# One weight piece of a mixture-of-experts stream loaded by nine transfers instead of one

## The reference

```python
def expert_block(args):
    xb, e = args
    g = xb @ w_gate[e] + b_gate[e]
    u = xb @ w_up[e] + b_up[e]
    g = jnp.minimum(g, SWIGLU_LIMIT)
    u = jnp.clip(u, -SWIGLU_LIMIT, SWIGLU_LIMIT)
    a = g * jax.nn.sigmoid(SWIGLU_ALPHA * g) * (u + 1.0)
    return a @ w_down[e] + b_down[e]
```

## Time and profile before

| what | us |
|---|---|
| median of 3 runs (1153.05 to 1154.56) | 1153.4 |
| the profiled execution, its own time | 1153.93 |
| the profiled execution, its span from first to last instruction | 1152.1 |
| TensorE busy in it (94% of the span) | 1081.1 |
| VectorE busy, ScalarE busy | 307.8, 212.9 |
| moved by DMA | 439.53 MB, mean 382 GB/s |

### The profile page before, as it was taken

How to read it: one execution, slowest core, us unless ns; L and a number is a source line. 1 busy time by engine, 2 the same in 40 slices (tenths; PEclk the granted TensorE clock), 3 DMA queues, 4 the chain that set the end, 5 groups by cost and what they waited for, 6 DMA issues and landing times.

```text
span 1152.1 us, 12104 instructions
## 1 busy us (share of the span) xinstructions
PE 1081.1 (94%) x5226; PEld 499.7 (43%) x5226; DVE 307.8 (27%) x690; ACT 212.9 (18%) x365; POOL 3.6 (0%) x11
## 2 busy tenths in 40 slices
PE   7999989999999999999999999999999898999997
PEld 6888879733333333333333333333333333333332
DVE  7566667531111112111111111111111111111122
ACT  5345445311111111111111111111111111000102
POOL 0000000000000000000000000000000000000000
PEclk9999999999999999999999999999999999999999
DMA  9754228799999999999999999999999999999995
GB/s 356 256 177 153 108 76 318 332 416 427 428 427 428 427 428 427 428 427 428 428 427 428 428 427 427 428 428 427 428 428 427 427 427 428 429 428 427 428 427 240
DMA packets 44858, 439.53 MB, mean 382 GB/s; under 512 B 3946, under 2 KB 5506, under 8 KB 20228
## 3 DMA queue, kind: packets, MB, share of 16 engines
q1 hardware_dynamic: 44788, 438.74, 91.2%
q10 hardware_dynamic: 16, 0.00, 0.0%
HBM read 437.68 MB, written 1.05 MB: 381 GB/s over the span
## 4 chain that ended last, share of the span: by engine, by line
PE 62%; DMA 31%; DVE 3%; issue 2%; ACT 1%; SPq 0%; DVEq 0%; ACTq 0%
PE ps L1006 37%; DMA pool<-in_w_up_dram 23%; DMA pool<-in_w_down_dram 4%; DMA attn<-in_w_up_dram 4%; PE ps L665 4%; PE ps L1028 3%; PE ps L937 3%; PE ps L695 2%; PE ps L746 2%; PE ps L703 2%; PE ps L993 1%; PE ps L799 1%; PE ps L801 1%; PE ps L800 1%; DMA wu<-in_w_in_dram 1%
## 5 line engine op out<-in xcount | busy, mean ns | idle before, releaser
L1006 PE MATMUL ps<-pool,o_t 128*64 128x512 f32 x2144 | 482.6, 596 | 31.9 <-DMA pool<-in_w_gate_dram 12.0
L1006 PEld LDWEIGHTS ps<-pool,o_t 128*64 128x64 f32 x2144 | 153.6, 137 | 319.2 <-issue 275.4
L1438 DVE TENSOR_SCALAR v_tok<-ps 128x512 f32<-128x512 f32 x32 | 22.1, 692 | 504.3 <-PE ps L1006 504.3
L1006 PE MATMUL ps<-attn,o_t 128*64 128x512 f32 x320 | 72.5, 594 | 4.1 <-DMA attn<-in_w_gate_dram 3.4
L599 ACT ACTIVATE o_t<-ps 128x512 f32<-128x512 f32 x32 | 19.1, 597 | 305.7 <-PE ps L665 305.6
L606 ACT ACTIVATE attn<-ps 64x512 f32<-64x512 f32 x60 | 35.5, 591 | 217.1 <-PE ps L1006 216.4
L1006 PE MATMUL ps<-slot_wv,o_t 128*64 128x512 f32 x304 | 69.4, 598 | 4.3 <-issue 2.2
L1006 PE MATMUL ps<-slot_gt,o_t 128*64 128x512 f32 x304 | 69.4, 598 | 4.3 <-issue 2.2
L586 ACT ACTIVATE attn<-v_tok 128x512 f32<-128x512 f32 x32 | 20.2, 630 | 243.1 <-DVE v_tok L1438 243.1
L1028 PE MATMUL ps<-attn,o_t 128*128 128x512 f32 x128 | 60.3, 594 | 0.8 <-DVE attn L1506 0.8
L937 PE MATMUL ps<-xs,work 128*64 128x512 f32 x256 | 60.7, 593 | 0.2 <-DVE work L1374 0.2
(11 more groups left out here) (190 smaller groups left out, 962.9 us busy)
## 6 DMA issues: line engine op xcount, KB each, us to landing
pool<-in_w_gate_dram SPq DMA_DIRECT2D x45, 2048.0 KB, 39.3
pool<-in_w_up_dram SPq DMA_DIRECT2D x45, 2048.0 KB, 39.4
pool<-in_w_down_dram SPq DMA_DIRECT2D x44, 2048.0 KB, 39.4
attn<-in_w_gate_dram SPq DMA_DIRECT2D x7, 2048.0 KB, 39.5
slot_wv<-in_w_up_dram SPq DMA_DIRECT2D x7, 2048.0 KB, 37.2
slot_gt<-in_w_down_dram SPq DMA_DIRECT2D x7, 2048.0 KB, 42.9
slot_gt<-in_w_up_dram SPq DMA_DIRECT2D x6, 2048.0 KB, 34.5
attn<-in_w_down_dram SPq DMA_DIRECT2D x6, 2048.0 KB, 38.3
```

Of the source, the lines that this page charges most:

```text
L1006: mm = pe.matmul(ps[SLOTS * h:SLOTS * h + SLOTS, bank, :], lhs[:, k, :], ring[n % RING][:, r, 512 * h:512 * h + 512], start=(k == 0 and no ...
L1438: dve.tensor_scalar(g_act, ps[:, G, :], LIMIT, None, ALU.min).then_inc(g_ready, 1)
```

## The change

Piece 96 is loaded by nine transfers in place of one: one of 64 partitions, then eight of 8 partitions each, all on SyncE's queue, into the same slot and with the same semaphore. The bytes and their places are the same. Each of the nine raises the semaphore by 16, so this slot's semaphore goes up by 144 for piece 96 instead of 16, and the waits for piece 96 and for all later pieces of slot 6 ask for 128 more. No other piece, and nothing on TensorE, VectorE or ScalarE, is changed.

```diff
+        EVEN_OUT = 96
+
+        def landed(n):
+            return 16 * (n // RING + 1) + (16 * 8 if n % RING == EVEN_OUT % RING and n >= EVEN_OUT else 0)
+
...
+                elif n == EVEN_OUT:
+                    expert, m, j = ORDER[n]
+                    sp.dma_start(ring[n % RING][0:P // 2], expert_v[m][expert, j, 0:P // 2]).then_inc(ld_ring[n % RING], 16)
+                    for p in range(P // 2, P, 8):
+                        sp.dma_start(ring[n % RING][p:p + 8], expert_v[m][expert, j, p:p + 8]).then_inc(ld_ring[n % RING], 16)
...
-                        pe.wait_ge(ld_ring[n % RING], (n // RING + 1 if again is None else again + (n // RING + 1)) * 16)
+                        pe.wait_ge(ld_ring[n % RING], landed(n) if again is None else again * 16 + landed(n))
```

## The result

The kernel with piece 96 in nine transfers takes 1168.32 us (median of 4 runs, 1168.09 to 1169.37), against 1153.98 us of the kernel before on the same chip: ratio 1.0127, 95% interval 1.0111 to 1.0143. I had predicted 1153.0, range 1151.6 to 1155.9, and 0.14 for slower by more than 2.3 us. It is 14.3 us slower by the medians, 14.7 by the ratio.

What follows compares the result with a forecast made beforehand. The landing of the last pieces through the full DMA queue was taken as the bound. All other terms being 0, 1153.93 - 0.35 = 1153.6 us profiled, 0.53 above the median, gave 1153.05, stated as 1153.0; range 1151.6 to 1155.9.

Steps and rivals of the forecast that it cites:

- What bounds the kernel: End of the kernel: landing of the last weight pieces sets it, through a full DMA queue moving 428 GB/s.
- Where the bytes go: Piece 96: one half of the engines carries 12 packets, the other 4, where both carried 8.
- Four packets at 26.7 GB/s, 2.45 us: From piece 96 on: four packets, 65.5 KB, shift one half of the engines 2.45 us earlier, the other 2.45 us later.
- Which half is late?: End of the stream: narrow transfers' engines were taken to be ahead, so piece 96 relieves the late half; -0.35 us, chance 0.58.
- one spot at the beginning: At 27.3 us, narrow transfers follow a 2 MB one; the engines they use were ahead, those left out last.
- the prediction's own last sentence: Wrong if engine lag isn't kept from 680 us, or if the slowest engine at the end is one narrow transfers use.
- The rival: End of the stream: the late half gets the bytes and ends 2.45 us later, time 1155.85; chance 0.18.
- -0.35 us: End of the stream: late engines relieved, but an early-half straggler becomes slowest, 1140.1 to 1139.75; range -0.8 to 0.
- Nine issues fit, the queue doesn't run dry: SyncE at piece 96: nine issues, 2.95 us, fit in 3.43 us and can't empty the queue; 0 us.
- Piece 96 itself, 0 us: Piece 96's use at 675.22: it lands up to 2.45 us later, any TensorE wait replacing a later one; 0 us.

Runs made afterwards that it cites:

- twice is twice: Pieces 96 and 126 each loaded in two transfers of 64 neighbouring partitions, against the kernel before: ratio 1.0150, cost 17.3 us.
- 64 or 32 neighbours: Piece 96 in two transfers of 64 neighbouring partitions, or four of 32, against the kernel before: ratio 1.0067 or 1.0081.
- every 8th: Piece 96 in eight transfers of 16 partitions, each taking every 8th of all 128, against the kernel before: ratio 1.0068, cost 7.8 us.
- every 4th of all 128: Piece 96 in four transfers of 32 partitions, each taking every 4th, against the kernel before: ratio 0.9998, cost 0 us.
- the run with 16 neighbours: Piece 96 in eight transfers of 16 neighbouring partitions, against the kernel before: ratio 1.0093, cost 10.7 us.
- free loadings: Piece 96 in four every-4th transfers, or only its lower half in eight narrow every-4th transfers, against the kernel before: ratio 0.9998 or 1.0005.
- eight column pieces: Piece 96 in eight transfers of all 128 partitions, 512 columns of one row each, against the kernel before: ratio 1.0010, cost 1.2 us.

## Why the prediction was wrong, point by point

*What bounds the kernel* held: the stream of pieces sets the end, what it loses at piece 96 is lost for good, and twice is twice.

*Where the bytes go* held in the count: from 640 to 700 us the kernel after has 226 packets under 512 B, 16 for each of its 10.1 pieces and 64 more, as one for each of eight engines in each of the eight narrow transfers makes.

*Four packets at 26.7 GB/s, 2.45 us* is the step that failed. It priced a packet by the engine alone and took for granted that an engine writes at the same rate to whatever partition. The trace of before had no transfer in the full stream that wasn't spread over all 128 partitions, so nothing there showed another price. A price that the trace doesn't show has to be bounded from both sides; a lower rate for the 64 neighbours and for the narrow ones belonged in the range, and I had put it at nothing. Measured: the rate fell from 427 to 226 GB/s for 21 us, and 10.2 of the 14.7 us are lost rate.

The Trainium skill had the rule, and I had looked past it: "SBUF — State Buffer", section "Door 1: The DMA port swizzle (why `[64,N]` ≈ `[32,N]`)", says that the rate depends on how many of 16 ports the partitions of a transfer reach, that 4 neighbours share a port with the 4 that lie 32 further, and that 64 neighbours reach no more ports than 32. By it 64 or 32 neighbours, and every 8th, reach half of the ports and every 4th of all 128 reaches all; the runs agree (7.4 to 8.0 us lost against 0, the dip at 197 to 249 GB/s of 427). A quarter of the ports should be slower still, and the run with 16 neighbours (8.8 us) says hardly. In the free loadings each engine can have a port by itself; in all costly ones several have to meet at one. That is how the runs read together with the page; no view names engines or ports, so it is argued, not shown.

*Which half is late?* Read from one spot at the beginning, and half right. Most late engines are relieved by the change, but the latest is one that gets the four packets; by the prediction's own last sentence that alone makes it wrong. The rival said that one such engine is enough, and so it was: in place of -0.35 us the distance of the last engine from a level end grew by 3.3 us in the change. Its price, 2.45 us, was near. I gave it 0.18, and it came on top of the loss of rate, which I hadn't at all.

*Nine issues fit, the queue doesn't run dry* held, and for far more than was asked: 27 us of issues cost 1.2 us (0 to 2.2).

*Piece 96 itself, 0 us*: TensorE waited 8 us for it, in place of later waits, as I had argued; the price was in the stream.

Left open: whether it is the writing side alone, which no run parts from reading over the whole piece; why bytes of the pieces beside piece 96 slow down too; why a quarter of the places is hardly worse than a half (engines at work on different ones of the eight transfers at one time would reach more places; no run tests it); what makes half of the engines late by the end; and why the narrow transfers of the upper half lose about as much by neighbours as by every 4th (10.3 or 9.4 us) while in the lower half it is 5.4 or 0. A gentler levelling isn't in sight: if the places belong to the engines as argued above, each narrow transfer that takes bytes off the other eight engines has to write their partitions.

## What to carry to other kernels

Keep every transfer of a DMA-bound stream spread over all 128 partitions; if a piece has to be cut, cut its columns, or take every 4th partition, not blocks of neighbours: the same four transfers cost 9 us or nothing. Every 8th isn't enough, it costs 7.8 us. In the profile look at the DMA share and the GB/s together: here a share of 1 with half the GB/s was a stream at half its speed with no engine idle. And before bytes are moved between engines to level an end, show that the latest engine is among those relieved; one that isn't takes the whole gain.

## What the runs showed of the hardware

- A cut of one 2 MB piece of 439.53 MB into two halves of 64 neighbouring partitions slows the whole queue to half its rate for 15 us (two halves, 197 to 249 GB/s), and the cut of the change for some 20 us (mean 226 GB/s); cut by every 4th partition it goes on at 427 GB/s.
- Transfers of 8 partitions use eight engines (64 completion packets for eight of them), and by every 4th partition of the lower half they don't slow the stream (428 GB/s over all), while by every 4th of the upper half they do (374 GB/s from 640 to 700 us).
- With some 40 us of work in the queue one issue on SyncE can take 4.2 us (median of the eight column pieces, the longest 6.6), where whole pieces take 0.33; all eight together cost 1.2 us (0 to 2.2).
